# Hybrid encoder, expert layer: GpSimd issues the U gather two slots ahead of the V gather

## What is computed

```
a   = gelu(u[idx] . x) * g        # idx: 8 heads x 16 experts for each token
out = sum over the experts of a * v[idx]
```

## Time and profile before

| | |
|---|---|
| Median of 3 runs | 3809.72 us (3805.19 to 3812.08) |
| Span of the profiled execution | 3811.5 us |
| Busy: PE / DVE / POOL / ACT | 81% / 45% / 45% / 26% |
| Mean DMA rate over the span | 326 GB/s |
| U gathers, V gathers | 512 and 512, 1.049 MB each |

### The profile page before, as it was taken

One profiled execution on the slowest core, in us unless ns is written; L12 is line 12 of the kernel. 1 busy time (PEld: TensorE's weight loads), 2 busy tenths in 40 slices (PEclk: granted clock), 3 DMA queues, 4 the chain that ended last, 5 costly groups with the idle time before them and its releaser, 6 DMA issues.

```text
span 3811.5 us, 33124 instructions
## 1 busy us (share of the span) xinstructions
PE 3089.0 (81%) x9272; PEld 1715.4 (45%) x9272; DVE 1726.9 (45%) x3093; ACT 1009.5 (26%) x2401; POOL 1697.6 (45%) x1145
## 2 busy tenths in 40 slices
PE   7888788888867777777699998788888877777777
PEld 6445644444423322222577876644444433222232
DVE  3333255555545555555311121255555555555554
ACT  3334322222212222221144443222222222222221
POOL 4003455444434444444177665455444444444443
PEclk8877999999988999999699998899999999999999
DMA  4113599999999999999178683599999999999998
GB/s 156 58 58 118 173 417 416 417 417 417 407 415 390 405 413 410 410 411 414 48 170 163 158 147 122 199 417 416 417 417 417 408 387 411 409 411 408 411 406 367
DMA packets 253041, 1242.05 MB, mean 326 GB/s; under 512 B 25888, under 2 KB 63264, under 8 KB 120864
## 3 DMA queue, kind: packets, MB, share of 16 engines
q0 software_dynamic: 147456, 1073.81, 68.3%
q1 hardware_dynamic: 105504, 167.23, 15.9%
HBM read 1238.85 MB, written 2.10 MB: 326 GB/s over the span
## 4 chain that ended last, share of the span: by engine, by line
PE 29%; DMA 28%; issue 23%; DVE 9%; POOL 9%; ACT 2%; SPq 0%; POOLq 0%; DVEq 0%; ACTq 0%
DMA room<-in_peer_u_dram,index 26%; PE psum L906 18%; POOL w_low L545 6%; PE psum L840 3%; POOL room L566 2%; PE psum L628 2%; PE psum L629 2%; PE psum L630 2%; DVE room L1671 2%; DMA room<-in_peer_v_dram,index 1%; ACT diag L1236 1%; POOL room L561 1%; DVE work L1646 1%; DVE work L1650 1%; DVE key_f L1652 1%
## 5 line engine op out<-in xcount | busy, mean ns | idle before, releaser
L906 PE MATMUL psum<-room,diag 128*128 128x512 f32 x4096 | 1939.4, 623 | 593.5 <-ACT diag L1236 584.2
L1671 DVE CUSTOM_DVE_ANT_0 room<-room,normed 128x2048 f32<-128x2048 f32 x512 | 1186.0, 2325 | 1195.0 <-DMA room<-in_peer_u_dram,index 1194.0
L906 PEld LDWEIGHTS psum<-room,diag 128*128 128x128 f32 x4096 | 789.5, 199 | 1667.5 <-issue 947.5
L566 POOL DMA_INDIRECT room<-in_peer_v_dram,index x512 | 571.2, 1116 | 1111.3 <-PE psum L906 560.9
L561 POOL DMA_INDIRECT room<-in_peer_u_dram,index x512 | 643.4, 1257 | 420.0 <-DVE dots L1671 191.2
L545 POOL TENSOR_TENSOR w_low<-wbuf,w_high 128x2048 fp32r<-128x2048 f32 (+1 forms) x108 | 480.8, 4462 | 556.5 <-ACT w_high L982 556.4
L1227 ACT ACTIVATE acts<-dots 128x1 f32<-128x1 f32 x512 | 103.8, 203 | 1903.2 <-DVE dots L1671 1903.2
L982 ACT ACTIVATE w_high<-wbuf 128x2048 fp32r<-128x2048 f32 (+1 forms) x108 | 200.4, 1859 | 279.7 <-DMA wbuf<-in_fox_w_in_dram 142.3
L628 PE MATMUL psum<-w_high,x_high 128*128 128x512 f32 (+1 forms) x608 | 242.5, 399 | 4.3 <-POOL w_low L545 4.3
L629 PE MATMUL psum<-w_low,x_high 128*128 128x512 f32 (+1 forms) x608 | 237.9, 391 | 0.0
L630 PE MATMUL psum<-w_high,other 128*128 128x512 f32 (+1 forms) x608 | 237.9, 391 | 0.0
(11 more groups left out here) (164 smaller groups left out, 1939.6 us busy)
## 6 DMA issues: line engine op xcount, KB each, us to landing
wbuf<-in_fox_w_in_dram SPq DMA_DIRECT2D x64, 1024.0 KB, 7.7
wbuf<-in_peer_w_q_dram SPq DMA_DIRECT2D x64, 512.0 KB, 15.5
wbuf<-in_mla_w_o_dram SPq DMA_DIRECT2D x16, 1024.0 KB, 5.1
wbuf<-in_fox_w_o_dram SPq DMA_DIRECT2D x16, 1024.0 KB, 5.1
wbuf<-in_mla_w_in_dram SPq DMA_DIRECT2D x8, 1024.0 KB, 8.2
wbuf<-in_mla_w_kvb_dram SPq DMA_DIRECT2D x32, 256.0 KB, 3.3
room<-in_peer_u_dram,index POOLq DMA_INDIRECT x512, 15.4
room<-in_peer_v_dram,index POOLq DMA_INDIRECT x512, 14.3
```

The source lines that it names most:

```text
L566: pool.indirect_dma_start(v_ring[:, r, :], None, peer_v.rearrange("l n d -> (l n) d"), bass.IndirectOffsetOnAxis(index[:, p, s:s + 1], 0)) ...
L906: mm = pe.matmul(psum[:, 4 * b + q, :], diag[:, r, :], v_ring[:, r, q * TILE:(q + 1) * TILE], start=False, stop=False, skip_group_check=True)
L1671: V.tensor_tensor_reduce(u_ring[:, r, :], u_ring[:, r, :], normed[:, b, :], 1.0, 0.0, ALU.mult, ALU.add, dots[:, r:r + 1]).then_inc(dot_do ...
```

## The change

GpSimd's order within the gathers is turned: in front of V of slot s it now issues U of slot s+2 (LEAD = 2), also across the units, where it waits for the next unit's `index_ready` in front of U of the next unit's slot 0. A layer begins with U0 and U1, and its last unit ends with V14 and V15 on their own. Waits, rings, indices, DMAs and their number are as before; the stream becomes U0, U1, U2, V0, U3, V1, and so on.

```diff
@@ -63,6 +63,7 @@
 CHOOSE_AT = 11
 COPY_Q_AT = 4
 CHOOSE_STEPS = 24
+LEAD = 2
 
 
 class Events:
@@ -549,22 +550,42 @@
                 with pool.Fori(0, tiles) as i:
                     low_parts([n0 + i])
 
-            def gathers(layer, number, p):
-
-                pool.wait_ge(index_ready, number + 1)
+            def gather_u(number, p, s):
+
+                pool.wait_ge(dot_done, number * SLOTS + s + 1)
+                pool.sem_inc(held["pool"], 1)
+                pool.indirect_dma_start(u_ring[:, s % RING, :], None, peer_u.rearrange("l n d -> (l n) d"),
+                                        bass.IndirectOffsetOnAxis(index[:, p, s:s + 1], 0)).then_inc(u_full[s % RING], 16)
+
+            def gather_v(number, p, s):
+
+                pool.wait_ge(mm_done, number * SLOTS + s + 1)
+                pool.sem_inc(held["pool"], 1)
+                pool.indirect_dma_start(v_ring[:, s % RING, :], None, peer_v.rearrange("l n d -> (l n) d"),
+                                        bass.IndirectOffsetOnAxis(index[:, p, s:s + 1], 0)).then_inc(v_full[s % RING], 16)
+
+            def gathers(number, p, more=True):
+
+
                 for s in range(SLOTS):
-                    r = s % RING
-                    slot = number * SLOTS + s
-
-                    pool.wait_ge(dot_done, slot + 1)
-                    pool.sem_inc(held["pool"], 1)
-                    pool.indirect_dma_start(u_ring[:, r, :], None, peer_u.rearrange("l n d -> (l n) d"),
-                                            bass.IndirectOffsetOnAxis(index[:, p, s:s + 1], 0)).then_inc(u_full[r], 16)
-
-                    pool.wait_ge(mm_done, slot + 1)
-                    pool.sem_inc(held["pool"], 1)
-                    pool.indirect_dma_start(v_ring[:, r, :], None, peer_v.rearrange("l n d -> (l n) d"),
-                                            bass.IndirectOffsetOnAxis(index[:, p, s:s + 1], 0)).then_inc(v_full[r], 16)
+                    if s + LEAD < SLOTS:
+                        gather_u(number, p, s + LEAD)
+                    elif more:
+                        if s + LEAD == SLOTS:
+                            pool.wait_ge(index_ready, number + 2)
+                        gather_u(number + 1, 1 - p, s + LEAD - SLOTS)
+                    gather_v(number, p, s)
+
+            def layer_gathers(first):
+                pool.wait_ge(index_ready, first + 1)
+                for s in range(LEAD):
+                    gather_u(first, 0, s)
+                pairs = NB * PHEADS // 2
+                with pool.Fori(0, pairs - 1) as i:
+                    for p in range(2):
+                        gathers(first + 2 * i + p, p)
+                for p in range(2):
+                    gathers(first + 2 * (pairs - 1) + p, p, more=p == 0)
 
             for t, width in enumerate((Q_RANK, KV_RANK, ROPE)):
                 low_parts([S_IN + t], width)
@@ -572,9 +593,7 @@
                 if layer:
                     low_parts_looped(S_FOX, 4 * fox.groups)
                 low_parts_looped(S_O[layer], 4)
-                with pool.Fori(0, NB * PHEADS // 2) as i:
-                    for p in range(2):
-                        gathers(layer, layer * NB * PHEADS + 2 * i + p, p)
+                layer_gathers(layer * NB * PHEADS)
```

## The result

The changed kernel takes 3783.9 us in the median of 4 runs (3779.8 to 3787.9), before 3809.9: a ratio of 0.9933, 95% interval 0.9919 to 0.9947, or 26 us (20 to 31). Faster, as forecast, inside the range of 3758 to 3798, by two thirds of the 38 us forecast. The profiled execution has a span of 3780.0 us and is among the shortest of its kernel's, that of before among the longest; the two traces differ by 31.5 us.

What follows compares the result with a forecast made beforehand. The queue of gathers, 422 GB/s undisturbed, was taken as the bound, with 55 us of gaps. 33.4 - 1.3 + 5.1 + 2.7 - 1.2 = 38.7 us off the 3811.5 span gave 3772.8; forecast 3772 us, range 3758 to 3798.

Steps and rivals of the forecast that it cites:

- Block 1: Gaps behind 14 expert choices in block 1, 15.5 + 17.9 us over both layers: all 33.4 us should go.
- U15 at its place without a gap: Behind a block 1 choice, U15 could land at 21.7 us after U10's landing, due at 24.9: no gap.
- Plain slots: Slots without a choice: six to eight gathers stay in flight in either order, so the change is worth 0.
- Block 0, bare units: Three block 0 choices without weight loads: gaps of 3.4 to 3.5 us replace 3.0, 3.3 and 2.6; cost 1.3 us.
- The delay of the choice: Block 0, units 0 to 6: the match behind mm8 makes `pick` late, so the choice starts 6.6 us late.
- Block 0, loaded units: Eleven block 0 choices beside weight loads: 2.1 MB queued covers the late U15, margin 1.5 us; cost 0, bounds 0 and 3.4 each.
- Change of block: From block 0 to block 1: a gap of 3.8 us replaces 6.5 and 6.2, gain 5.1 us; bounds +12.7 and -1.3.
- End of layer 0: GpSimd's subtractions catch only the dot of 15: gain 2.7 us; about 0 if 14 is caught too, 16 if none.
- End of layer 1: V13 to V15 land 2.5 us apart but cost PE 3.5 each, so the last matmul ends later: cost 1.2 us.
- The estimate from the Trainium skill: Alternative from a DMA fixed cost of about 2.0 us: five remaining gaps 1.1 us shorter each, sum 5 us lower; not adopted.
- the row: Profile reading used for late issues: with nothing queued, a gather landed 5.6 us after the start of a 0.94 us issue.

Runs made afterwards that it cites:

- The late addition: Changed kernel (LEAD = 2) with block 0's PSUM addition into resid moved behind the first six units of block 1: 3773.5 us, ratio 0.9903 to before.

## Why the prediction was right, and what was mis-sized

The direction and the mechanism held: a V gather that waits for matmuls at a low clock, with a U gather behind it, made the gaps. The traces differ by 31.5 us, the sum was 38.7, and the medians by 26 for the 38 forecast. By its terms, counted as before by the rates of the windows:

- **Block 1, 33.4 us.** Right in full: 422 GB/s and a clock of 1.00 in both layers. U15 at its place without a gap was the step it hung on.
- **Plain slots, 0.** Right. The page's DMA issues give 16.2 and 15.1 us from issue to landing for U and V, 15.4 and 14.3 before: a slightly fuller queue.
- **Block 0, bare units, -1.3 us.** The mis-sized term: -6.8 (15.7 us of gap for 8.9), and one more in unit 6 of layer 0, where FOX weights were to cover it (367 GB/s over 15 us, 2.0 us for about 1). The delay of the choice was right, 6.9 us for 6.6. What failed was the step from a late landing to a gap: "U15 is issued at 21.5 and lands at 28.4, due is 24.9: a gap of 3.4 to 3.5". The landing itself was right within 0.3 us: of the two U gathers in this stretch and the V between, the trace gives

```profile
L557 POOL DMA_INDIRECT room<-in_peer_u_dram,index x2: 1911/2060/2208, 970.5 to 975.2; - x2
...
DMA to landing us min/median/max: 6.9/7.8/8.7
```

```profile
L564 POOL DMA_INDIRECT room<-in_peer_v_dram,index x1: 1907/1907/1907, 973.0 to 973.0; - x1
...
DMA to landing us min/median/max: 8.4/8.4/8.4
```

  The 6.9 is U15's. It lands at 977.4, 6.3 us behind V12 (957.27 + 13.8 = 971.1) where 2.5 is the pace: 3.8 us late. V13 behind it, issued 2.5 us later beside the next dot, took 8.4, and lands 4.0 us behind U15: 1.5 us more, which I had not counted, since I let everything behind the first late gather follow at the pace of the stream. U16 follows 2.5 us behind V13. That makes 5.3 us by landings for the 5.0 by rate. But the second delay is no idle stretch of the DMA:

```profile
968.00:975.00 7.00, 4.30 (x7) 1.95 (x8) 7.00 (x7) 2.63 (x9) 4.12 (x2) 0.58 0.44 146
...
977.40:981.40 4.00, 2.00 (x5) 0.57 (x3) 2.30 (x2) 0.90 (x3) 3.39 (x3) 1.00 1.02 391
```

  4.6 of the 5.0 us are missing in the first window, which opens 3 us before V12 has landed, and only 0.3 between the landings of U15 and V13, where 1.56 MB moved, half as much again as one gather. The transfers thus overlap: the rate fell before the last queued gather had landed, and when U15 landed, 3.8 us late, the stream had already lost 4.6. The step took the one for the other.
- **Block 0, loaded units, 0 within 0 and 3.4 each.** Right on average: 416 and 417 GB/s over 420 and 400 us in the two layers, before 417 and 416, and 85.6 us from choice to choice, as before. Right by a small margin: LEAD = 3 turned it into the largest loss.
- **Change of block, +5.1 us.** +3.8: gaps of 5.1 and 3.8 for a computed 3.8 each. The second late landing is in the trace here too: behind U20, issued at 1172.56 and 6.9 us under way, V18 lands 3.7 us later (1175.07 + 8.1), in layer 1 3.9 (3139.17 + 7.0, 3141.68 + 8.4). In layer 1, 1.5 of the 3.8 us stand behind the choice of unit 7, where I had U15 with time to spare. The late addition confirmed the cause of the rest.
- **End of layer 0, +2.7 us.** +4.0. V15, issued at 1790.58, lands 10.8 us later at 1801.3, the addition begins 17.2 us after it and 21.2 before. The dot of 14 escaped, as assumed.
- **End of layer 1, -1.2 us.** -1.1: the addition begins 5.8 us behind V15's landing (3757.42 + 10.3) for 4.7.

These come to 32.3 us for the 31.5 measured, a closer match than the readings deserve. From the first landing to the last the gathers of layer 0 take 1338.8 us before and 1326.6 after, those of layer 1 1333.9 and 1320.0: 26.1 us, where the terms by rate give 29.4 (33.4 - 6.8 - 1.0 + 3.8). And 1.7 of the 31.5 us lie ahead of the first gather, where nothing was changed. That the forecast gain held to two thirds rests on block 1; the smaller terms are known to some 3 us together.

The medians differ by 26 us, as the profiled executions lie at opposite ends of their kernels' runs. What makes the runs of one kernel differ by 7 to 12 us, with LEAD = 2 above all, no run here tells. Part of it stands ahead of the change: in the two traces of the changed kernel the first gather is issued at 466.1 and at 460.4 us, and yet the spans differ by 1.1 us only.

The estimate from the Trainium skill, "DMA: Bandwidth & Descriptors", section "Anatomy of one DMA" (a fixed cost of about 2.0 us), would have put U15's gap 1.1 us lower. The trace sides with the row: U15 took 6.9 us as computed from 5.6, and the next gather 8.4.

## What to carry to other kernels

When one in-order queue issues two streams, the lead of one over the other moves a wait rather than removing it: price what hangs on the delayed stream too, here a match three engines away, for each slot of lead, and take the smallest lead that closes the gaps. Look at both ends of a bandwidth-bound stretch: one more wait on GpSimd and one addition moved gave 11 and 12 us, each nearly half of what the reordering gave. And where a gather goes out late, count the landings of the two or three behind it as well, and read the loss of the stream from the DMA rate, which falls before the last gather in the queue has landed.

## What was not expected of the hardware

A 1 MB gather issued into an empty queue landed 5.6 us after its issue; issued one after another beside running dots, three took 6.9, 8.4 and 8.7 us, the last with a transfer in front of it. The instructions account for 1.0 to 1.3 us of the difference (1.9 to 2.2 us of issue for 0.94); the rest of V13's 8.4 came after its issue had ended, 6.5 us for 4.7. In the 4.0 us before it landed the DMA engines moved 1.56 MB, so part of that went to gathers behind it. Why V13 waited on them was not tried.
